# The router of a two-layer transformer: tokens turned without their norm, its scale and shift folded into weights and bias, the second gate's products moved among the heads, a mask applied as a limit

## What is computed

```python
for l in range(2):
    mod = silu(c) @ mod_w[l] + mod_b[l]            # six rows of 1024
    shift1, scale1, gate1, shift2, scale2, gate2 = split(mod, 6)
    h = rms_norm(x, norm1_g[l]) * (1 + scale1) + shift1
    mix = diff_fox_mixer(h, ...) if l % 2 == 0 else stick_breaking_mixer(h, ...)
    x = x + gate1 * mix
    h = rms_norm(x, norm2_g[l]) * (1 + scale2) + shift2
    x = x + gate2 * hier_moe(h, ...)               # 4 groups x 8 experts

# hier_moe: the router
g_prob = softmax(h @ w_gr + b_gr)                  # 4 groups, the best one is taken
e_logits = (h @ w_er + b_er)[of the best group]    # 8 experts, the best two are taken
# every expert: silu(h @ w1) * (h @ w3) @ w2, weights 1024x512, 1024x512, 512x1024

# stick_breaking_mixer (layer 1), 16 heads, mask = key strictly before query
log_keep = where(mask, log_sigmoid(-z), 0)
later = reverse_cumsum(log_keep) - log_keep
a = where(mask, exp(log_sigmoid(z) + later), 0)
o = a @ v
```

## Time and profile before

| | |
|---|---|
| median of 3 runs | 1285.79 us |
| the profiled execution | 1282.9 us, of which 1281.2 us are the span |
| PE busy | 923.9 us (72%) |
| DVE, ACT, POOL busy | 313.6, 204.0, 33.7 us |
| read from memory | 488.25 MB, 382 GB/s over the span |
| layer 0: dense and route stage, expert stage | 0 to 215.9 us, 215.9 to 650 us |
| layer 1: the same | 650 to 840.8 us, 840.8 to 1281.2 us |

### The profile page before, as it was taken

One profiled execution on the slowest core, in us unless ns is written; L12 is line 12 of the kernel. 1 busy time (PEld: TensorE's weight loads), 2 busy tenths in 40 slices (PEclk: granted clock), 3 DMA queues, 4 the chain that ended last, 5 costly groups with the idle time before them and its releaser, 6 DMA issues.

```text
span 1281.2 us, 13563 instructions
## 1 busy us (share of the span) xinstructions
PE 923.9 (72%) x5563; PEld 431.8 (34%) x5563; DVE 313.6 (24%) x617; ACT 204.0 (16%) x423; POOL 33.7 (3%) x97
## 2 busy tenths in 40 slices
PE   7999999566565647465889998967374665765568
PEld 3444545122121213131366765533131212222223
DVE  1578634001010101010156565421010101101011
ACT  2213414010110001000120552420010101010000
POOL 4000000000000000000000121000000000000000
PEclk9999999778787878687999997998796878878879
DMA  9997878999999999999999822889999999999997
GB/s 358 349 388 270 335 289 335 416 429 428 426 430 429 427 429 429 427 428 427 415 399 380 328 97 106 337 354 429 428 428 428 429 428 428 429 428 427 428 424 297
DMA packets 73455, 489.97 MB, mean 382 GB/s; under 512 B 17964, under 2 KB 18100, under 8 KB 46528
## 3 DMA queue, kind: packets, MB, share of 16 engines
q1 hardware_dynamic: 73104, 488.25, 92.4%
q10 hardware_dynamic: 304, 1.07, 0.2%
HBM read 488.25 MB, written 1.05 MB: 382 GB/s over the span
## 4 chain that ended last, share of the span: by engine, by line
DMA 51%; PE 38%; DVE 6%; SPq 2%; issue 2%; ACT 1%; DVEq 0%; ACTq 0%
DMA tokens<-in_moe_w_dram 45%; PE bank L1064 12%; PE bank L793 5%; PE bank L1093 5%; PE bank L973 5%; PE bank L846 4%; DMA ring<-in_moe_w_dram 3%; DMA ring<-in_mod_w_dram 3%; SPq L491 2%; PE bank L720 2%; DVE alone L1640 1%; PE bank L913 1%; PE bank L929 1%; PE bank L1033 1%; PE bank L1027 1%
## 5 line engine op out<-in xcount | busy, mean ns | idle before, releaser
L1064 PE MATMUL bank<-ring,region 128*32 128x512 f32 x1456 | 266.5, 679 | 170.2 <-DMA tokens<-in_moe_w_dram 91.8
L1093 PE MATMUL bank<-ring,region 128*32 128x512 f32 x832 | 144.8, 721 | 139.4 <-DMA ring<-in_moe_w_dram 84.5
L1064 PEld LDWEIGHTS bank<-ring,region 128*32 128x32 f32 x1456 | 69.9, 123 | 351.7 <-issue 291.0
L1064 PE MATMUL bank<-work,region 128*32 128x512 f32 x256 | 138.3, 703 | 0.0
L1064 PE MATMUL bank<-tokens,region 128*32 128x512 f32 x256 | 138.2, 703 | 0.0
L1988 DVE TENSOR_TENSOR region<-region,bank 128x512 f32<-128x512 f32 x16 | 11.0, 688 | 445.3 <-PE bank L1064 445.3
L1093 PEld LDWEIGHTS bank<-ring,region 128*32 128x32 f32 x832 | 37.2, 129 | 232.5 <-issue 193.8
L793 PE MATMUL bank<-ring,tokens 128*128 128x512 f32 x256 | 114.1, 596 | 0.6 <-ACT tokens L1293 0.6
L1998 DVE TENSOR_TENSOR region<-bank,region 128x512 f32<-128x512 f32 x32 | 22.1, 692 | 271.1 <-PE bank L1093 271.1
L1293 ACT ACTIVATE region<-bank,shift,scale 128x128 f32<-128x128 f32 x64 | 24.1, 457 | 367.9 <-PE bank L1051 367.9
L1051 PE MATMUL bank<-region,h 128*128 128x128 f32 x512 | 63.4, 285 | 8.7 <-issue 7.9
(11 more groups left out here) (262 smaller groups left out, 986.7 us busy)
## 6 DMA issues: line engine op xcount, KB each, us to landing
ring<-in_moe_w_dram SPq DMA_DIRECT2D x140, 2048.0 KB, 19.3
work<-in_moe_w_dram SPq DMA_DIRECT2D x22, 2048.0 KB, 24.0
tokens<-in_moe_w_dram SPq DMA_DIRECT2D x22, 2048.0 KB, 28.5
ring<-in_mod_w_dram SPq DMA_DIRECT2D x20, 2048.0 KB, 15.4
ring<-in_od_w_in_dram SPq DMA_DIRECT2D x5, 2048.0 KB, 15.1
ring<-in_mod_w_dram SPq DMA_DIRECT2D x8, 1024.0 KB, 14.4
ring<-in_ev_w_in_dram SPq DMA_DIRECT2D x4, 2048.0 KB, 17.8
ring<-in_moe_w_dram SPq DMA_DIRECT2D x6, 1024.0 KB, 18.3
```

The costliest lines, as they stand in the source:

```text
L1064: last = pe.matmul(bank[which][32 * j:32 * j + 32, :], m.seated[:, k, 32 * j:32 * j + 32], weights(4 * which + j, k * FE), start=(k == 0), ...
L1093: last = pe.matmul(bank[half][32 * j:32 * j + 32, :], m.hidT[:, c, 32 * j:32 * j + 32], w, start=(c == 0), stop=(c == FC - 1), skip_group_ ...
```

## The change

Five things are done.

1. The router reads the turned tokens of x itself, without norm. The router's weights are multiplied once for each layer by the scale (DVE, `scale_router`), the shift times the weights is summed to a bias (`router_bias` on PE, `copy_bias` on DVE), and the logits are multiplied by the token's reciprocal root and the bias added when DVE takes them from PSUM. So the turn waits for x alone (`turn_rows`, `norm_rows`), and the 16 pieces of modulation become four plain copies of 512 columns.
2. The products of gate 2 move from behind the last projection into the steps of `attend` (14 and 15 in layer 0, twice 13 in layer 1); their weights are loaded ahead of the output weights.
3. Scale and shift of the second norm are finished earlier: steps 12 and 13 in layer 0, 2 and 4 in layer 1, where the sums move from step 12 to step 1, in PSUM bank 5.
4. POOL no longer masks. The tile strict holds 0 and -1e30 in place of 1 and 0, and DVE takes the smaller of it and -z, so that masked positions get an exponential of 0.
5. The first expert loads go where the second gate's products free slots, and the spare loads stand two places later in layer 0's order (`ALONE_AT`, `APART_AT`).

```diff
-LAST_DENSE = [("out", 0), ("out", 1), (GATE2, 0), (GATE2, 1)]
+GATE_THEN_OUT = [(GATE2, 0), (GATE2, 1), ("out", 0), ("out", 1)]
...
+LATE_SUMS_BANK = 5
...
-ALONE_AT = 1
-APART_AT = 2
-SECOND_PART_AT = (14, 12)
-SECOND_COLS_AT = (15, 14)
-ADD_SUMS_AT = (17, 12)
+ALONE_AT = (3, 1)
+APART_AT = (4, 4)
+SECOND_PART_AT = (12, 2)
+SECOND_COLS_AT = (13, 4)
+GATE2_AT = ((14, 15), (13, 13))
+ADD_SUMS_AT = (17, 1)
...
-    for hh in range(NHH):
-        pool.wait_ge(m.s["sb_exp"], hh + 1)
-        pool.tensor_tensor(m.pr[hh % 2][:, :], m.pr[hh % 2][:, :], m.strict[:, :], ALU.mult).then_inc(
-            m.s["sb_masked"], 1)
...
                 if l == 1:
-                    pe.wait_ge(s["sb_masked"], w + 1)
+                    pe.wait_ge(s["sb_exp"], w + 1)
...
+            if step == GATE2_AT[l][0]:
+                mod_products(l, GATE2, 0)
             if step == O_TURN_AT[l]:
                 turn_half(l, 0)
+            if step == GATE2_AT[l][1]:
+                mod_products(l, GATE2, 1)
...
         for i in range(4):
             project_out(l, 1, i)
+            if i == 0:
+                router_bias(l)
...
+    def router_bias(l):
+
+        pe.wait_ge(s["router_scaled"], l + 1)
+        b = bank[2][:, COL - LOGITS:COL]
+        pe.matmul(b, m.ones[:, 0:P], m.shift_sum, start=True, stop=False, skip_group_check=True)
+        pe.matmul(b, m.ones[0:1, 0:P], m.r_b[0:1, l, :], start=False, stop=True, skip_group_check=True).then_inc(
+            s["bias_made"], 1)
+
+    def turn_rows(l):
+
+        pe.wait_ge(s["bias_ready"], l + 1)
+        pe.wait_ge(s["part_ready"], PARTS[l][GATE2])
+        for t in range(TT):
+            pe.wait_ge(s["x_added"], TT * 2 * l + t + 1)
+            for k in range(KC):
+                last = pe.transpose(row_turned_at(bank, k, t), m.x[:, t, k:D:KC], m.ident[:, :])
+            last.then_inc(s["hT_turned"], 1)
+
     def route(l):
-        mod_row(l, GATE2, 0)
-        pe.wait_ge(m.got["router"], 16 * ROUTER_LOADS)
         for t in range(TT):
...
-                pe.matmul(b, m.hT[:, k, t * P:(t + 1) * P], m.r_w[:, l, k, :], start=(k == 0), stop=False)
-            last = pe.matmul(b, m.ones[0:1, 0:P], m.r_b[0:1, l, :], start=False, stop=True)
+                last = pe.matmul(b, m.hT[:, k, t * P:(t + 1) * P], m.r_w[:, l, k, :], start=(k == 0), stop=(k == KC - 1),
+                                 skip_group_check=True)
         last.then_inc(s["routed"], 1)
-        mod_row(l, GATE2, 1)
+        mod_row(l, GATE2, 0)
...
         last.then_inc(s["x_placed"], 1)
+        pe.wait_ge(s["logits_moved"], TT * (l + 1))
+        mod_row(l, GATE2, 1)
...
-        for e in range(2):
-            mod_products(l, GATE2, e)
-        turn_tokens(2 * l + 1)
+        turn_rows(l)
...
+    def norm_rows(l):
+
+        act.wait_ge(s["x_added"], TT * 2 * l + 1)
+        chain.link(fn(m.h[:, 0, :], m.x[:, 0, :], ACT.Square, accum_out=m.sq_sum[:, 0:1]))
+        chain.link(inverse_root(m.sq_sum[:, 0:1], m.rstd[:, 0:1], D))
+        copy_rows_turned(l, 0, 0)
+        act.wait_ge(s["x_added"], TT * 2 * l + 2)
+        chain.link(fn(m.h[:, 1, :], m.x[:, 1, :], ACT.Square, accum_out=m.sq_sum[:, 1:2]))
+        copy_rows_turned(l, 1, 1)
+        inverse_root(m.sq_sum[:, 1:2], m.rstd[:, 1:2], D).then_inc(s["rstd_done"], 1)
...
     def route(l):
+        chunk_rows(l)
         copy_row(l, 2)
-        chunk_rows(l)
...
         add_out(0, 0, 3)
+        scale_router(0)
         mod_cols(1, FIRST)
+        copy_bias(0)
+        mod_part(0, GATE2)
+
+    def scale_router(l):
+
+        dve.wait_ge(m.got["router"], 16 * ROUTER_LOADS)
+        w = m.r_w[:, l, :, :]
+        shifted = m.tmp2[:, 0:KC * LOGITS].rearrange("p (k n) -> p k n", k=KC)
+        link(tt(shifted, w, wide(m.shift[:, :], LOGITS), ALU.mult))
+        link(dve.tensor_reduce(m.shift_sum, shifted.rearrange("p k n -> p n k"), AX_X, ALU.add))
+        tt(w, w, wide(m.scale[:, :], LOGITS), ALU.mult).then_inc(s["router_scaled"], 1)
...
-        link(ts(keep, z, -SCALE, 0.0, ALU.mult, ALU.min))
+        link(stt(keep, z, -SCALE, m.strict[:, :], ALU.mult, ALU.min))
...
-        norm_first_tile(2 * l + 1)
-        mod_part(l, GATE2)
-        modulate(2 * l + 1)
+        for t in range(TT):
+            dve.wait_ge(s["hT_turned"], TT * (2 * l + 1) + t + 1)
+            half = 1 - t
+            dve.tensor_copy(rows_turned(m, t, half),
+                            bank[2 * (1 - t) + half][:, :].rearrange("p (k t) -> p k t", k=4)).then_inc(s["hT_dve"], 1)
...
+        dve.wait_ge(s["rstd_done"], 2 * l + 2)
...
+            stt(logits[:, t, :], bank[2][:, LOGITS * t:LOGITS * (t + 1)], m.rstd[:, t:t + 1], m.bias, ALU.mult,
+                ALU.add).then_inc(s["logits_moved"], 1)
```

More of the change, by code:

```diff
@@ L279, in allocate @@
     m.first_g = m.normed[0][0:KC, 0:P]
+    spare = [m.att[:, 2 * D + LOGITS * i:2 * D + LOGITS * (i + 1)] for i in range(2)]
+    m.shift_sum, m.bias = spare
+    m.logits = m.att[:, 2 * D + 2 * LOGITS:2 * D + 4 * LOGITS].rearrange("p (t n) -> p t n", t=TT)
     m.sc, m.pr, m.pT = ([m.att[:, i * ATT:(i + 1) * ATT] for i in pair] for pair in ((0, 1), (2, 3), (4, 5)))
@@ L568, in program_pool @@
     pool.memset(m.pick[:, :, :], 0.0).then_inc(step, 1)
-    for tile, value in ((m.upper, 1.0), (m.above, 1.0), (m.causal, 0.0), (m.strict, 1.0)):
+    for tile, value in ((m.upper, 1.0), (m.above, 1.0), (m.causal, 0.0), (m.strict, 0.0)):
         pool.memset(tile[:, :], value).then_inc(step, 1)
@@ L1238, in row_bank @@
 def row_bank(group, half):
[L1240 removed]
+    return 2 if group == GATE1 else 3 - half
 def weights_of(l, hh):
@@ L1328, in modulate @@
         scale, shift = modulation(m, n)
-        for out, k, t in turned_pieces(m, n, ks):
-            act.wait_ge(s["hT_turned"], TT * n + (TT if t is None else t + 1))
-            fn(out, turned_at(bank, n, k, t), ACT.Identity, scale=scale[:, k:k + 1],
+        for out, k in turned_pieces(m, ks):
+            act.wait_ge(s["hT_turned"], TT * n + TT)
+            fn(out, turned_at(bank, n, k, None), ACT.Identity, scale=scale[:, k:k + 1],
                bias=shift[:, k:k + 1]).then_inc(s["hT_act"], 1)
@@ L1519, in program_scalar @@
         copy_turned_half(l, 1)
-        norm(2 * l + 1)
-        modulate(2 * l + 1)
+        norm_rows(l)
         route(l)
@@ L1583, in mod_part @@
             wait_dense(dve, m, l, MOD_AT[l][group][-1])
-        out, b = m.part, bank[3 if l == 1 else mod_bank(group)]
+        out, b = m.part, bank[late_bank(group) if l == 1 else mod_bank(group)]
         if group == FIRST:
@@ L1699, in modulate @@
         scale, shift = modulation(m, n)
-        for out, k, t in turned_pieces(m, n, ks):
-            dve.wait_ge(s["hT_turned"], TT * n + (TT if t is None else t + 1))
-            ts(out, turned_at(bank, n, k, t), scale[:, k:k + 1], shift[:, k:k + 1],
+        for out, k in turned_pieces(m, ks):
+            dve.wait_ge(s["hT_turned"], TT * n + TT)
+            ts(out, turned_at(bank, n, k, None), scale[:, k:k + 1], shift[:, k:k + 1],
                ALU.mult, ALU.add).then_inc(s["hT_dve"], 1)
@@ L1868, in attend_odd @@
         add_out(1, 0, 3)
+        mod_part(1, GATE2)
+        scale_router(1)
+        copy_bias(1)
     def copy_out(half):
```

80 lines of the change are left out of this document (48 added, 32 removed).

## The result

The changed kernel takes 1272.51 us, the median of 4 runs (1271.38 to 1274.02), against 1285.99 us for the kernel before, measured beside it (1285.33 to 1286.63): a ratio of 0.9895, 95% interval 0.9882 to 0.9907, 13.5 us less. Measured again later it was 1273.49 us (1272.50 to 1276.31), ratio 0.9905 (0.9891 to 0.9920). One single run of the kernel before there took 4937 us and is left out of the ratios. The forecast was 1276.2 us. The profiled execution took 1274.02 us with a span of 1272.3; before it was 1282.9 and 1281.2, so the two profiles differ by 8.9 where the forecast was 9.6. The 4.6 us between the two ways of counting are taken up further down.

What follows compares the result with a forecast made beforehand. Expert stages are memory-bound, so the time follows when each layer's first expert unit is used: 0.0 gained in layer 0 and 9.6 in layer 1, 1285.8 - 9.6 = 1276.2 us; own range 1273.5 to 1279.5, wider range 1271 to 1283.

Steps and rivals of the forecast that it cites:

- What bounds the kernel: Memory bounds the unchanged expert stages; ahead of them DMA runs dry, so only earlier R0 and R1 shorten the time.
- R0: Moment layer 0's first expert unit has been used and loading goes on; 223.01 us before, forecast to move by 0.0.
- R1: Moment layer 1's first expert unit has been used and loading goes on; 847.85 us before, forecast 9.6 earlier.
- The route stage: Both layers, from T to the ranks: 13.4 us in place of 17.17, a gain of 3.7 in each, bounds 2.0 to 5.4.
- T: The prediction's mark for the end of the last projection ahead of the route stage, 192.87 us in layer 0 before.
- Layer 0 ahead of T: Gate 2's products, 3.6, go into a full queue; with small terms T comes 3.7 us later, cancelling the route stage's gain.
- within 1 us of 223.0: Sign that the forecast is right: where R0 should lie; a move of more than 1.5 would be wrong.
- Layer 1 ahead of T: Gate 2's products hide in step 13's waits and step 14 keeps full clock: T 5.9 us earlier.
- the row: Profile row giving 120 ns a record for bias and router products, held to against the skill page's 25 ns.
- low clock in step 13: Rival: layer 1's clock falls there all the same, only the route stage's 3.7 less 0.5 remains, 1282.5 us; chance 0.15.
- DMA limit: Rival "Nothing": DMA was the limit after all, R1 gains some 2 us, 1284 us; chance 0.08.
- The slower rival: PE's clock is low from the turn to the ranks, losing 9.4 us in each layer, 1295 us; chance 0.07.

Runs made afterwards that it cites:

- experiment 7: The change with gate 2's products of layer 1 in step 17 in place of step 13; ratio to the kernel before 0.9957, 1280.78 us.
- experiment 8: The change with gate 2's products of layer 0 in step 17 in place of 14 and 15; ratio to the kernel before 0.9912, 1273.62 us.
- experiment 9: The change with POOL's mask restored (0/1 mask, POOL multiplication for each head); ratio to the kernel before 0.9918, 1275.9 us.
- experiment 10: The change with one of the four products that place x moved between the turns of the two token tiles; ratio to the kernel before 0.9898, 1273.4 us.
- Experiment 11: The change with one product that places x moved between the turns, plus four empty products in layer 0's step 13; ratio to the kernel before 0.9885, 1270.98 us.
- experiment 3: The kernel before with 11 empty products ahead of layer 1's half turn in step 13, filling one wait; ratio 0.9983, 1283.0 us.
- experiment 4: The kernel before with 11 empty products ahead of layer 1's half turn and 8 behind it, filling both waits; ratio 0.9978, 1282.25 us.
- experiment 5: The kernel before with the change's schedule alone (gate 2's products, loads, columns, sums); norm, modulation, router and POOL's mask as before; ratio 1.0019, 1289.03 us.
- experiment 1: The kernel before, unchanged, timed and profiled once more; ratio 1.0005, 1286.53 us.
- experiment 6: The kernel before with the moved schedule alone, plus 10 and 4 empty products in the route stage's two waits; ratio to the kernel before 0.9984, 1283.87 us.

## Why the prediction was right

**What bounds the kernel** held: R0 and R1 were the right marks, DMA is empty ahead of both, and behind R1 nothing changed.

**The route stage.** Forecast: ranks 13.4 behind T, the start of the next product. Measured by that mark: 13.2 (197.90 to 211.06), 4.0 less than the 17.17 of before, rather than 3.7. Counted from the end of the projection, as in the experiments, it is 13.0 in both layers (and 13.0 twice when repeated) against 17.1. The clock falls once in this leg, as assumed: L781 at 1.52 and L1056 at 4.92. In the ten legs of experiments 7 to 11 it was 11.4, from the projection's end, seven times, with no low clock in it, and 12.1 or 13.0 three times, with one; the forecast's bound for a leg without was 11.8. Experiment 9 has the change's route stage line for line and 11.4 in both layers, so which of the two comes differs between executions. DVE's decision came at T + 11.5, forecast T + 11.7.

**Layer 0 ahead of T** was the term that was mis-sized: forecast +3.7, measured +5.0 (197.90 against 192.87). The step of the prediction that set the wait of 1.56 ahead of step 14's scores against 1.10 of column products, and left it at that, missed the clock. The waits of 0.20 and 0.86 are followed by low clock at 153.5: from step 14's scores to the turn behind them it takes 2.87 (153.56 to 156.43), where it took 1.52 before. That is 1.35, all of the difference. Experiment 11, which fills the second wait, takes it away: T is at 196.64, +3.8, the forecast term. (Its R0, 221.24, owes 1.6 more to a route stage without low clock.) Step 15's projection starts 4.6 later (163.40 against 158.79), where the prediction's sign was about 3, for the same reason. So R0 came out at 224.03, on the edge of "within 1 us of 223.0", and in the repeat at 226.10, which by the prediction's own sign (moved by more than 1.5) would have counted against it. That the first profile fell inside was in part luck. Over four profiles with the change's layer 0 (experiments 7 and 9 and the change's two) R0 averages 224.2, over five with that of before 224.3: no shift can be told, so the forecast of 0.0 holds as an average, not for one execution.

**Layer 1 ahead of T.** Counted from R0, step 6's scores start 0.04 earlier (forecast 0.1), step 14's 1.3 earlier (forecast 1.3) and step 15 starts 6.5 earlier (forecast 6.4), the clock at 770 is full, and L975 takes 3.65. From R0 to the end of the last projection it is 588.8 in place of 594.8, 6.0 less against a forecast of 5.9; from R0 to R1 10.1 less against 9.6. L1848's successor stands at 0.56 in all 16 heads, as the prediction's sign asked. The half of this that the prediction argued from a row alone (a full clock in step 14 if its waits are filled) is what experiments 3, 4 and 7 test: one wait filled is not enough, both are, and empty products do it for 3.9 us.

**Small terms.** The bias products take 0.57 in layer 0 and wait for nothing (forecast 0.5), the hole between the turns is 0.68 (0.6), and the router's 32 records take 3.66 (3.8). By the Trainium skill, "VectorE: DVE Perf Modes", section on the TRN2 errata, the estimate for the router was 0.8 (32 records of 25 ns); the measured 3.66 decides for the row.

**The rivals.** A low clock in step 13 and a DMA limit did not appear. The slower rival did not appear either, but layer 0 of experiment 5 is that rival made real: the schedule without the folded norm is a small loss. The prediction argued against it by the dense placing of x; the run shows that this alone doesn't keep the clock: it came back only at 220.3, behind 17 us at half. What differs in the change is the short wait, 0.68, ahead of the router; that this is what protects it fits all 14 legs, but was not tested by itself, since the folded router also has fewer products.

**The time.** By the profiles the change gives 8.9 us, by the medians 13.5 and 12.5. The prediction took 2.9 us, the distance of one profile of before from its median, as a constant of both kernels. It isn't one: the first profile of before, 1282.9, lies below every timed run of before (lowest 1283.39, highest 1288.93), and the profile of the change, 1274.02, is the highest of its own four runs. A second pair of profiles gives 1283.88 and 1276.05, 7.8 apart. The sum's two parts were off in opposite ways in the first pair: R0 +1.0 where 0.0 was forecast, R0 to R1 -10.1 where it was -9.6. Single executions of a kernel lie up to 5.5 us apart, of which R0 accounts for 2.5 in the profiles (experiment 1). An execution of before near 1288 was never profiled. With the average R0 of either kernel (224.3 and 224.2, above) in place of one profile's, the gain by the profiles would be an estimated 10.2 us, so 2 to 3 us of the medians' gain have no place in any trace. Where they lie stays open, and so does whether the change is less exposed to them: its nine runs (1271.4 to 1276.3) spread about as widely. That the median came 3.7 us below the forecast of 1276.2 is this open part; by the profiles the sum itself was 0.7 too good.

**Where the gain comes from**, by the runs: the route leg gives 4.1 in each layer, spent again in layer 0 (T later by 5.0, of which 3.6 is gate 2's products). In layer 1, of 6.0 ahead of T, 2.2 is POOL's mask (experiment 9), and the place of gate 2's products decides over 6.5 (experiment 7). Ahead of T in layer 1 the parts add up: the schedule alone gives 3.9 (experiments 5 and 6: 590.8 and 591.0 in place of 594.8), the mask 2.2, together the 6.0. Over the whole kernel they don't: the mask alone gives 0.12%, the schedule alone loses 0.19% (in its profile, in layer 0's route stage), and together with the folded norm they give 1%.

## What to carry to other kernels

Work that moves off the critical path must go into a wait: in a full queue it costs what it cost before (layer 0), in a wait it is free and can keep the clock up (layer 1: 6.5 us for 3.6 us of products). Ask first what the work was covering where it stood; here its old place hid the norm, and the move paid over the whole kernel only together with the edit that removed that wait. Before an edit is judged by one profile, take a second of the same kernel: here the shift between two was up to 2.5 us in a part that no edit had touched.

## What the runs showed of the hardware

With only the first of two waits that stand close together filled, the clock fell 7 us later and the projection behind took 5.95; with both, 3.70. PE was busy for the whole of two windows of 4 us at half clock (experiment 5), and the dearest thing behind a wait of 2.35 was not the wait but the 17 us of low clock that followed it. The same waits in layer 1 of the same execution were followed by none: a wait makes a fall possible, not certain, so one profile does not settle what a wait costs. Empty products in a wait are a real tool: 14 in each layer's route stage took 4.5 us off the schedule alone (experiment 6).
